# One block for norm, projection and decay tables: the column blocks unrolled and reordered, the channel norm moved into the delta-rule scan

## What is computed

```
n1 = _rmsnorm(h, g_mix)
proj = n1 @ w_in                      # q,k,v (1536), z (512), b (4), a (4), glu (1024)
qkv = silu(causal_depthwise_conv(qkv, w_conv_qkv))        # 4 taps
beta = sigmoid(b_raw)
g = -exp(a_log) * softplus(a_raw + dt_bias)
o = gated_delta_rule_chunked(q, k, v, g, beta)            # tables exp(gc_i - gc_j), exp(gc)
o = o * rsqrt(mean(o * o) + EPS) * g_gdn_out * silu(z)
u = glu_in + b_glu
u = u[..., :512] * sigmoid(u[..., 512:])
c = causal_depthwise_conv(u, w_conv_dw) + b_conv_dw       # 31 taps, 512 channels
y_conv = silu(layernorm(c, ln_conv_g, ln_conv_b))         # over the 512 channels
mix = concat(o, y_conv)
```

## Time and profile before

| | |
|---|---|
| median of 3 runs | 1433.52 us (1433.09 to 1434.51) |
| the profiled execution's own time | 1430.73 us |
| its span in the profile | 1429.0 us, mean granted TensorE clock 0.895 |
| busy | PE 82%, DVE 44%, ACT 23%, POOL 17% |
| norm, until the first projection matmul | 0 to 36.05 us |
| projection loop and small columns | 36.05 to 323.4 us |
| decay tables and channel statistics | 323.9 to 364.9 us |
| scan | 365.1 to 574.1 us |
| from there to the end | 855 us |

### The profile page before, as it was taken

How to read it: one execution, slowest core, us unless ns; L and a number is a source line. 1 busy time by engine, 2 the same in 40 slices (tenths; PEclk the granted TensorE clock), 3 DMA queues, 4 the chain that set the end, 5 groups by cost and what they waited for, 6 DMA issues and landing times. The chain is left out here.

```text
span 1429.0 us, 17466 instructions
## 1 busy us (share of the span) xinstructions
PE 1171.8 (82%) x6337; PEld 776.2 (54%) x6338; DVE 626.0 (44%) x886; ACT 325.0 (23%) x691; POOL 246.1 (17%) x341
## 2 busy tenths in 40 slices
PE   4999999998588777799539788778898877748997
PEld 3888888896377666688413233233333322316775
DVE  7398989883464664532441111111111111144553
ACT  5221221203454343322101010100010110032222
POOL 2100000002446553000112111111121111011111
PEclk7999999976688999899669999999999998978998
DMA  4212111100000010421479999999799999962221
GB/s 150 60 44 59 44 44 44 44 0 0 1 2 2 1 61 2 141 89 59 190 310 421 427 425 424 422 418 406 284 427 426 427 420 415 404 222 81 96 96 44
DMA packets 68059, 272.67 MB, mean 191 GB/s; under 512 B 11625, under 2 KB 38442, under 8 KB 51370
## 3 DMA queue, kind: packets, MB, share of 16 engines
q1 hardware_dynamic: 56096, 254.30, 44.5%
q0 software_dynamic: 9456, 16.80, 3.1%
q10 hardware_dynamic: 2458, 0.92, 0.3%
HBM read 264.12 MB, written 25.43 MB: 203 GB/s over the span
## 5 line engine op out<-in xcount | busy, mean ns | idle before, releaser
L2123 PE MATMUL ps_u<-wup,xgT 128*64 128x512 f32 x1024 | 257.1, 660 | 61.2 <-DMA wup<-in_w_up_dram 58.8
L2123 PEld LDWEIGHTS ps_u<-wup,xgT 128*64 128x64 f32 x1024 | 85.5, 151 | 231.1 <-issue 229.9
L93 PE MATMUL ps_b<-n_hi,wh 128*128 128x512 f32 x384 | 150.3, 391 | 6.1 <-DVEq L406 6.1
L93 PE MATMUL ps_b<-n_lo,wh 128*128 128x512 f32 x384 | 150.0, 391 | 0.0
L93 PE MATMUL ps_b<-n_hi,wl 128*128 128x512 f32 x384 | 149.9, 390 | 0.0
L2043 DVE TENSOR_TENSOR hb<-sil,ps_u 128x256 f32<-128x256 f32 x32 | 13.5, 421 | 298.3 <-ACT sil L1983 298.3
L93 PEld LDWEIGHTS ps_b<-n_hi,wh 128*128 128x128 f32 x384 | 72.5, 189 | 21.6 <-ACTq L41 6.5
L93 PEld LDWEIGHTS ps_b<-n_lo,wh 128*128 128x128 f32 x384 | 72.5, 189 | 15.2
L93 PEld LDWEIGHTS ps_b<-n_hi,wl 128*128 128x128 f32 x384 | 72.4, 189 | 15.0
L1983 ACT ACTIVATE sil<-ps_u 128x256 f32<-128x256 f32 x32 | 12.3, 385 | 285.9 <-PE ps_u L2123 285.9
L424 DVE SCALAR_TENSOR_TENSOR convT<-upad,vecT,convT 128x1024 f32 (+1 forms) x60 | 76.8, 1280 | 0.0
(11 more groups left out here) (366 smaller groups left out, 2022.2 us busy)
## 6 DMA issues: line engine op xcount, KB each, us to landing
wup<-in_w_up_dram SPq DMA_DIRECT2D x64, 2048.0 KB, 17.4
zT<-in_w_down_dram SPq DMA_DIRECT2D x32, 1024.0 KB, 17.6
convT<-in_w_down_dram SPq DMA_DIRECT2D x32, 1024.0 KB, 19.1
wraw<-in_w_in_dram SPq DMA_DIRECT2D x25, 512.0 KB, 4.0
convT<-y_rows SPq DMA_DIRECT2D x16, 512.0 KB, 4.5
qkvT<-in_x_dram SPq DMA_DIRECT2D x8, 512.0 KB, 7.6
qkvT<-in_w_out_dram SPq DMA_DIRECT2D x8, 512.0 KB, 4.9
xr<-in_x_dram SPq DMA_DIRECT2D x8, 512.0 KB, 3.3
```

The source lines that it names most:

```text
L93: ins = nc.tensor.matmul(ps, lhs[a], rhs[b], start=first and k == 0, stop=last and k == 2)
L2123: last = nc.tensor.matmul(ps_u[k][HC[c], :], xgT[k][:, j, HC[c]], wup[k][c][:, j, :], start=j == 0, stop=j == NJ - 1)
```

## The change

The norm, the projection and the decay tables become one block with no common wait inside.

* *Norm.* The gain is multiplied in when the tile is scaled (`gB`, the gain broadcast over 128 partitions, 512 KB). The turned tile stays in PSUM and feeds high and low part directly, so `gained` is gone.
* *Early half blocks.* PE starts on the first halves (tokens 0 to 511) of the blocks g0 and u0 after five turned tiles, with the turns of tiles 5, 6 and 7 between them.
* *Projection.* 24 column blocks written out in the order g0 u0 q0 k0 g1 u1 v0 q1 k1 g2 u2 v1 q2 k2 g3 u3 v2 q3 k3 v3 z0 z1 z2 z3, with three weight slots in place of two. ACT makes the high weights of block b+3 before it drains block b. Channel 0's taps go in halves. Each place in DVE's taps where low weights are made is written out.
* *Small columns* are made after block v0, from a load of their own, and the chain to g runs within the taps of channel 1.
* *Decay tables* are made beside z2 and z3: `sums` on PE, `differences` at the end of DVE's work, `decays` on ACT before the drains of z2 and z3.
* *Channel norm.* Sums, centring, squares and roots are done in the scan, a pair at a time, in banks lent by the inverse. `norm_columns` and silu come a pair late; those of the last pair come after everything else in the scan.

The core of the diff (lines left out where "..."):

```
+        order = ["g0", "u0", "q0", "k0", "g1", "u1", "v0", "q1", "k1", "g2", "u2", "v1",
+                 "q2", "k2", "g3", "u3", "v2", "q3", "k3", "v3", "z0", "z1", "z2", "z3"]
+        bank = lambda b: b % 3
+        wslot = lambda b: b % 3 if b < NB - 1 else 0
+        wfree = lambda b: b - 2 if b < NB - 1 else b - 1
...
+                    nc.scalar.activation(n1[0][:, :, t * P:(t + 1) * P], ps_x[t % 2], ACT.Copy).then_inc(a_hi, 1)
...
+                def w_high(b):
+                    act.wait_ge(s_w[b % 2], 16 * (b // 2 + 1))
+                    if b >= 3:
+                        act.wait_ge(p_half[1], wfree(b))
...
+                for b in range(NB):
+                    if kind[b] == "z" and num[b] == 2:
+                        for t in range(NT):
+                            decays(t)
+                        act.wait_ge(*a_steps.sem_at(f"eg{NT - 1}"))
+                    if b + 3 < NB:
+                        w_high(b + 3)
+                    drain(b)
+                    if b == BA_AFTER:
+                        decay_inputs()
...
+                    nc.vector.scalar_tensor_tensor(xn[t % 2], xs[:, t, :], rs[:, t:t + 1], gB, ALU.mult, ALU.mult).then_inc(v_xn, 1)
...
+                ready(0)
+                part(0, 0, first_js)
+                turn(5)
+                part(0, 0, last_js)
+                ready(1)
+                part(1, 0, first_js)
+                turn(6)
+                turn(7)
+                part(1, 0, last_js)
...
+                part(0, 1, every)
+                part(1, 1, every)
...
+                sums(0)
+                sums(1)
+                block(NB - 2)
+                sums(2)
+                sums(3)
...
 # in the scan, VectorE
+                    if i:
+                        norm_columns(i - 1)
                     state(i, 0)
                     if ahead:
                         eliminate(i + 1, (4,))
+                    centred(i)
                     remainder(i, 1)
...
                     state(i, 1)
+                    mean_squares(i)
                     outputs(i)
+                norm_columns(NP2 - 1)
```

More of the change, by code:

```diff
@@ L145, in hybrid_block_kernel, with drains @@
+        p_steps = Steps(sem("pe_steps"), ["vecs", "ba", "gc"] + [f"E{t}" for t in range(NT)])
+        def drains(b):
+            return 2 * sum(k != "u" for k in kind[:b + 1])
+        p_half = [sem(f"pe_h{h}") for h in range(2)]
         with ExitStack() as c1:
@@ new lines, in _ @@
+                tap_sum(1)
+                w_low(10)
+                conv(2)
+                conv(3)
+                w_low(11)
+                conv(4)
+                summed_decays()
+                gated(2, 0)
+                gated(2, 1)
+                w_low(12)
+                dve.wait_ge(v_u, 6)
+                dve.wait_ge(v_tap, taps)
+                for k in range(KC):
+                    tap(2, k, slice(0, T))
+                    if k in (8, 16, 24):
+                        w_low({8: 13, 16: 14, 24: 15}[k])
@@ new lines, in _ @@
+                tap_sum(2)
+                w_low(16)
+                conv(5)
+                conv(6)
+                w_low(17)
+                conv(7)
+                gated(3, 0)
+                gated(3, 1)
+                dve.wait_ge(v_u, 8)
+                dve.wait_ge(v_tap, taps)
+                for k in range(KC):
+                    tap(3, k, slice(0, T))
+                    if k in (4, 12, 19, 27):
+                        w_low({4: 18, 12: 19, 19: 20, 27: 21}[k])
+                tap_sum(3)
@@ new lines, in drained, with part @@
+                def drained(b):
+                    if kind[b] == "u":
+                        pe.wait_ge(v_u, 2 * num[b] + 2)
+                    else:
+                        pe.wait_ge(a_drain, drains(b))
+                def part(b, h, js):
+                    w, ps = wslot(b), ps_b[bank(b)]
+                    for j in js:
+                        last = mm3(ps[:, h, :], [wh[w][:, j, :], wl[w][:, j, :]], [n1[0][:, j, HF[h]], n1[1][:, j, HF[h]]],
+                                   j == 0, j == NJ - 1)
+                    if js[-1] == NJ - 1:
+                        last.then_inc(p_half[h], 1)
@@ new lines, in sums @@
+                def sums(t):
+                    pe.wait_ge(*g_steps.sem_at(f"GT{t}"))
+                    if t == 1:
+                        pe.wait_ge(*v_steps.sem_at("ngc"))
+                    if t >= 2:
+                        pe.wait_ge(*v_steps.sem_at(f"dm{t - 2}"))
+                        pe.wait_ge(*a_steps.sem_at(f"eg{t - 2}"))
+                    nc.tensor.matmul(ps_E[t % 2], ones[:], GT[t % 2], start=True, stop=True).then_inc(*p_steps(f"E{t}"))
+                for t in range(5):
+                    turn(t)
@@ L692, in hybrid_block_kernel @@
-        G2 = range(2)
         NBK = P // BS
@@ L700, in hybrid_block_kernel @@
         NWO = 4
-        s_wo = [sem(f"s_wo{s}") for s in range(NWO)]
+        s_wo = s_x[0:NWO]
         wo_raw = [qkvT[:, NT + s, :] for s in range(NWO)]
@@ L1333, in _ @@
                     turn_out(i, 1)
+                    if not ahead:
+                        channel_rows(i)
         gdn.close()
+        tables.close()
         masks.close()
```

882 lines of the change are left out of this document (435 added, 447 removed).

## The result

The changed kernel takes 1396.24 us (median of 4 runs, 1395.64 to 1399.03), beside 1433.3 us for the kernel before on the same chip: ratio 0.976, interval 0.973 to 0.978, so 37 us faster. The forecast was 1399.5. The profiled execution took 1395.64 us; its span is 35.1 us shorter than that of before.

The account below looks back on a forecast made before the run. PE was taken to bound the projection loop, with DVE not far behind. From 1430.7 us, 40.7 less up to the scan and 6.6 more in it gave 1396.6, plus 2.8 to the median: 1399.5 us, range 1389 to 1413.

Parts of the forecast that it names:

- the bound of 29: Projection start: upper bound of 29 us if the broadcast gain in SP's queue delays every x tile; 23.2 was forecast.
- Clock at the start: First projection matmuls on PE: 3 us at clock 0.50, so 1.5 us lost.
- Q: Start of the second halves of the first blocks on PE, forecast at about 38.4 us; DVE's channel 0 timed from it.
- 24 blocks at 10.88: Projection on PE: each column block priced at 10.88 us from the earlier trace, 261.1 us in all.
- Small columns: After block v0 on PE: clock expected to fall again, 24.1 us, plus 1.5 for the block behind; at 1.00 throughout, 10 less.
- Rival 1: Clock stays at 1.00 in the small columns: 10 to 11.5 us less, 1388.5 us; chance 0.10.
- Waits for DVE: PE's waits for DVE's second gating and low weights before the scan, 1.7 us in all.
- Rival 2: DVE becomes the bound through late x and 2 us more per channel: 1411.5 us; chance 0.15, shared with the fifth rival.
- The product with two SBUF inputs: Scan on DVE: such products take 2.33 us when GpSimd works, 1.21 otherwise; products with a PSUM operand cannot be held up.
- Clock, 4.2 gained by filling the gap: Scan, between the solves: filled waits bring pair 0 to pair 2's pace and pair 1 gains 1.4; 4.2 us gained.
- rival 3: Scan pays half clock: 4.2 us not gained and sums of squares cost 3.4 each; +11, 1410.5 us; chance 0.12.
- Rivals 4 and 5: Half-clock blocks make it slower (five: 1454 us; 0.02); early start followed by equal wait, tables after z (1410; counted within 0.15).

Follow-up runs that it names:

- e1: Changed kernel with the early half blocks undone: projection begins only after all eight turned tiles and their low parts; 1406.99 us, ratio 0.981.
- e12: Changed kernel with the third weight slot moved next to the others and the raw weight buffers at SBUF's right end, same PSUM banks; 1396.35 us, ratio 0.976.
- e5: Changed kernel with the sums of squares of pairs 0 to 2 made between the two turns of the output tiles; 1399.28 us, ratio 0.978.
- e6: Changed kernel with the last pair's norm_columns and silu moved into the wait for POOL's root; 1396.74 us, ratio 0.979.
- e11: Changed kernel with the channel norm and its silu left out entirely; 1374.34 us, ratio 0.961.
- e8: Changed kernel with small columns' roles exchanged (wba as weights, n moving, rows turned back) and DVE's low weights from block 7 earlier; 1395.84 us, ratio 0.974.
- e7: Changed kernel with ACT draining block g0 before making the high weights of block 3; 1395.3 us, ratio 0.973.
- e2: Changed kernel with only 16 of 128 small-column matmuls left; 1394.51 us, ratio 0.975.
- e9: Changed kernel with the decay tables made after the last column block instead of beside z2 and z3; 1409.92 us, ratio 0.984.
- e10: Changed kernel plus five edits: small columns turned, raw weights at right end, g0 drained first, last pair's tail in root wait, squares between turns; 1378.16 us, ratio 0.963.
- the nine kernels: The changed kernel and eight edits of it with the same scan, which takes 216.7 to 224.2 us, mean 220.7.
- e3: Changed kernel with the third slot of high and low weights 32 bytes lower in SBUF; 1397.82 us, ratio 0.976.

## Why the prediction was right, step by step

The mechanism was right, but that the number came out so close is partly luck, since two misses of opposite sign nearly cancelled: the scan starts 3.4 us later than the 324.4 of the forecast, and the profiled scan is 4.4 shorter than its +6.6 (+2.2). The remaining 2.2 of the 3.3 us by which the median was overstated are the distance of median and profiled execution, 2.8 assumed, 0.6 found.

- *Start of the projection.* 22.89 for 23.2. The broadcast gain delayed nothing, so the bound of 29 was idle. e1 gives the worth of the overlap, 8.1.
- *Clock at the start.* "3 us at 0.50, so 1.5 lost" is mis-sized. The first 12 matmuls take 5.26 us instead of 2.7: 2.5 lost. The row of 23.46, 0.63 long, is followed by one 0.42 later. Turns 2.5 for 2.9. Q came at 39.15 for 38.4.
- *24 blocks at 10.88.* This step failed for seven of them: 11.24 each, 2.5 us in all. I took the price from a kernel that had no third slot, and did not ask where in SBUF the new one lies. e12 settles it. With the 1.0 above it is as large as the miss of 3.4; the other terms up to the scan nearly cancel.
- *Small columns.* 24.4 for 24.1. Other executions of the same stretch took from 22.3 to 25.2: from 105.73 to 128.18 in e5, 106.19 to 131.39 in e6. The clock falls sooner in some than in others: from 108 to 112 it is 0.89 in e5 and 0.57 in e6. This, and a slow start that ends up to 1.3 us sooner (105.63 for 106.90 at the first small matmul, in e11), moves the scan's start between 324.9 and 328.7, so the forecast's 324.4 was inside half a microsecond of the short ones for a partly wrong reason. Rival 1 fell: the clock was 0.50. The Trainium skill, "TensorE: Matmul & The Clock Gate", section "LDWEIGHTS (loading the stationary operand)", says that the time of loading weights goes by their columns, which makes 107 ns for 128 by its formula. The trace agrees: at full clock the small matmuls follow each other in 0.11 us (eight from 106.92 to 107.82), and with 16 columns of weights and 512 moving ones e8 does the same work in 7.4 us.
- *Waits for DVE.* 1.0 for 1.7 after the first (0.70), and DVE at Q + 9.1 for Q + 8.6. e7 shows that removing them brings 1.7 at most. Rival 2 fell in the changed kernel; but e2 and e8 show how near it was, at a place that I had not listed (the sum of g, 7.3 us of margin).
- *Tables beside z.* No wait of PE there, as said. Without that place it costs 7.2 more (e9). DVE's low weights and the first product of a short convolution are lengthened beside GpSimd's table products (298.98 to 302.0):

```profile
299.23 1.88 DVE L417 TENSOR_TENSOR wl<-wraw,wh 128x1024 fp32r<-128x1024 f32 x1 [5.14 <-ACT wh L267]
301.03 1.52 DVE L480 TENSOR_SCALAR qkvT<-cinv,vecT 128x1024 f32<-128x1024 f32 x1
```

  1.88 for 1.22 and 1.52 for 0.75, 1.4 us together, hidden by PE. The Trainium skill, "SBUF — State Buffer", section "Who interferes with whom", says that a DVE instruction with two SBUF inputs contends with a GpSimd instruction that reads SBUF, and that `tensor_scalar` can contend as well. The trace agrees, and the 1.4 us are below the 2 us that the prediction gave it.
- *The product with two SBUF inputs.* The prediction read the earlier trace rows as 2.33 us when GpSimd worked and 1.21 otherwise. That reading is wrong: in the kernel before GpSimd's products stand beside DVE's in pair 0 and in pair 2 as well, by POOL's timeline:

```profile
419.93 2.49 POOL L892 TENSOR_TENSOR ml<-LT,lev 128x512 f32<-128x512 f32 x2 [9.83 <-PE ps_gb L1147]
...
518.32 3.58 POOL L892 TENSOR_TENSOR ml<-LT,lev 128x512 f32<-128x512 f32 x2 [9.81 <-PE ps_gb L1147]
```

  In pair 0 GpSimd's two products take 2.49 us (one alone takes 1.27 at 382.85 after) and DVE's takes 2.33; in pair 2 GpSimd's take 3.58 and DVE's 1.21. So one of the two is held up, not always DVE. What followed from it held: the centrings, with one input in PSUM, take 1.21 us, in pair 0 (388.86) beside a GpSimd product that takes 1.28 (388.84).
- *Sums in the wait for R.* Right. From the read of the state to the solve of tile 0 it is 3.56, 3.99, 3.99 and 3.16 us instead of 5.35, 4.23, 4.22 and 1.94: 1.0 gained for 0.8.
- *Sums of squares.* 1.72 a pair for 1.7, right, and on the path. e10 shows that they need not be.
- *`norm_columns` and centring.* The overrun is 0.1 to 0.25 a pair (6.66 and 6.80 for 6.56; waits for R of tile 1 of 0.99 and 1.13 for 0.78), not the 0.5 a pair that the sum used.
- *Clock, 4.2 gained by filling the gap.* The size is right between the solves: 9.37 + 8.19 became 6.66 + 6.80, 4.1 gained. The reason is only half right. e11 keeps its clock in pair 0 with the gap empty, and with the gap filled the visits at half clock come in the stretch behind. In the changed kernel's own profile that stretch was slow once (1.6 us), in the nine kernels more often; their mean scan is 6.1 us longer than before's, where the forecast had +6.6. What made the profiled scan short lies elsewhere: in the stretches that the change hardly touches, from the scan's start to the first read of the state and from each pair's second turn to the next pair's read, it took 118.6 us and the kernel before 123.4 (the nine took 118.6 to 121.7, 120.0 in the mean). The windows view shows the last of them, before and after, at a granted clock of 0.90 and 1.00:

```profile
537.67:555.48 17.81, 14.75 (x308) 12.86 (x309) 11.26 (x25) 5.67 (x15) 7.58 (x7) 0.90 0.01 2
...
497.27:514.01 16.74, 13.30 (x309) 11.61 (x309) 10.57 (x24) 5.67 (x15) 8.85 (x9) 1.00 0.01 2
```

  These 4.8 us stood in no term of the forecast. So the profiled scan, at +2.2, was a lucky one, and rival 3 is in part true of the others. Before's scan was profiled once, so how lucky that one was stays open.
- *Tail.* +3.4 for +3.3, and e6 takes it back whole. With it the scan adds up: sums in the wait -1.0, solve to solve -4.0, sums of squares 6.9, the one slow visit 1.6, tail 3.4, the stretches just named -4.8, together +2.2.
- *Rivals 4 and 5.* No block at half clock, and no equal wait behind the early start.

## What to carry to other kernels

When a stretch of PE's work is shortened or moved, list everything whose deadline it carries, down to the smallest matmul: here the low weights had been moved in time and one 128x32 product, waiting for a chain of small DVE and ACT steps, took back 10 of 16 us. Size an added buffer by where it will lie, not only by whether it fits, and compare the pace of equal blocks in the new trace at once. Read an edit's worth from the stretch between two fixed instructions; a scan of waits and short matmuls varied by 7 us between executions, more than most of the edits here are worth.

## What was unexpected of the hardware

- Matmuls whose weights lie at 194,112 bytes and above in each SBUF partition (194,080 in e3) follow each other in 0.234 us, those whose weights end at 194,048 or below in 0.2267 (128x512, float32 in its fast form; the addresses are those of the built programs). A shift of 32 bytes changes nothing. Whether it is that region or its distance to the moving operand (103,904 to 169,440) stays open.
- The first 5.3 us of the projection run at half pace (0.43 us a matmul, and 1.95 us for eight turns against 1.05 later), while the granted clock is given as 1.00 there:

```profile
24.00:26.00 2.00, 2.00 (x6) 1.53 (x5) 2.00 (x2) 0.29 (x2) 1.66 (x7) 1.00 0.88 222
```

  Steps of 0.43 us are those of the kernel before at a granted clock of 0.50 (seven matmuls from 36 to 39 us), so this is the pace of the 1.2 GHz level. The granted clock of a row is not enough by itself at the start of a kernel; the step between matmuls is.
- In the full set of small columns, 128x16 and 128x8, the clock fell to 0.50 in every profiled execution, with PE never idle (0.50 from 110.5 to 131.3 after, from 306 to 323 before); in e8's 16x512 matmuls for the same products it stayed at 1.00.
